# Fillers at a layer boundary, adds moved up in a norm, first loads and last outputs dealt out anew, small columns by tokens

## The reference, cut to what matters

```python
for l in range(2):
    h = rms_norm(x, norm_mix[l])
    proj = h @ w_in[l]                      # 7688 columns; da, db are 4 + 4 of them
    (dq, dk, dv, dz, da, db, mq, mk, mv, lx, ly, gates) = split_columns(proj)
    mixed = g0 * y_deltanet + g1 * y_attention + g2 * y_recurrence
    x = x + mixed @ w_o[l]
    h = rms_norm(x, norm_ffn[l])
    gate, up = jnp.split(h @ ffn_in[l], 2, axis=-1)
    x = x + (jax.nn.silu(gate) * up) @ ffn_down[l]
return rms_norm(x, norm_final)
```

## Time and profile before

| | |
|---|---|
| time, median of 3 runs | 951.11 us (950.91 to 951.41) |
| the profiled execution's own time | 952.0 us |
| its span | 950.2 us |
| TensorE busy | 930.6 us, 98% |
| VectorE / ScalarE busy | 646.4 us / 495.0 us |
| mean granted TensorE clock | 0.994 |
| TensorE stopped on listed waits | 10.4 us in all |

### The profile page before, as it was taken

The page is one execution under the profiler, slowest core; times in us unless marked ns, Lnnn a source line. Parts: engine busy times, 40 slices in busy tenths (PEclk is TensorE's granted clock), DMA queues, the critical chain, the costliest instruction groups (busy, mean ns, idle before and its releaser), DMA issues.

```text
span 950.2 us, 15345 instructions
## 1 busy us (share of the span) xinstructions
PE 930.6 (98%) x6344; PEld 833.7 (88%) x6344; DVE 646.4 (68%) x1026; ACT 495.0 (52%) x837; POOL 2.4 (0%) x6
## 2 busy tenths in 40 slices
PE   7999999999999999999999999999999999999996
PEld 5999899999987888888879998999999788888885
DVE  6889956685767555555678897665858675555555
ACT  6574445775446444444465555467744454444442
POOL 0000000000000000000000000000000000000000
PEclk9999999999999999999999999999999999999999
DMA  8554424446554655565635344344555566555541
GB/s 300 181 169 139 134 93 134 151 161 199 184 188 151 205 189 187 178 200 177 212 127 181 121 139 133 95 149 149 188 178 178 177 199 203 191 183 183 179 146 45
DMA packets 43989, 158.65 MB, mean 167 GB/s; under 512 B 5008, under 2 KB 5264, under 8 KB 43920
## 3 DMA queue, kind: packets, MB, share of 16 engines
q1 hardware_dynamic: 43920, 157.67, 50.3%
HBM read 156.60 MB, written 1.05 MB: 166 GB/s over the span
## 4 chain that ended last, share of the span: by engine, by line
PE 88%; DVE 7%; ACT 3%; DMA 1%; issue 1%; SPq 0%; DVEq 0%; ACTq 0%
PE bank L293 12%; PE bank L294 11%; PE bank L295 11%; PE bank L391 8%; PE bank L389 8%; PE bank L390 8%; PE bank L466 6%; PE bank L333 5%; PE bank L331 5%; PE bank L332 5%; PE bank L431 2%; DVE wlo L984 2%; PE bank L432 1%; PE bank L433 1%; PE bank L404 1%; DVE tmp L1031 1%
## 5 line engine op out<-in xcount | busy, mean ns | idle before, releaser
L707 ACT CAST whi<-raw 128x1024 fp32r<-128x1024 f32 x292 | 305.9, 1050 | 361.0 <-PE bank L295 132.1
L984 DVE TENSOR_TENSOR wlo<-raw,whi 128x1024 fp32r<-128x1024 f32 x292 | 353.2, 1219 | 131.9 <-ACT whi L707 131.3
L293 PE MATMUL bank<-ahi,whi 128*128 128x256 f32 x832 | 239.5, 288 | 0.4
L294 PE MATMUL bank<-alo,whi 128*128 128x256 f32 x832 | 235.3, 283 | 0.0
L295 PE MATMUL bank<-ahi,wlo 128*128 128x256 f32 x832 | 235.3, 283 | 0.0
L293 PEld LDWEIGHTS bank<-ahi,whi 128*128 128x128 f32 x832 | 159.4, 192 | 2.0 <-DVE tmp L1031 0.5
L294 PEld LDWEIGHTS bank<-alo,whi 128*128 128x128 f32 x832 | 159.5, 192 | 0.1
L295 PEld LDWEIGHTS bank<-ahi,wlo 128*128 128x128 f32 x832 | 159.4, 192 | 0.0
L389 PE MATMUL bank<-whi,ahi 128*128 128x512 f32 x320 | 126.5, 395 | 0.0
L391 PE MATMUL bank<-whi,alo 128*128 128x512 f32 x320 | 124.8, 390 | 0.0
L390 PE MATMUL bank<-wlo,ahi 128*128 128x512 f32 x320 | 124.5, 389 | 0.0
(11 more groups left out here) (243 smaller groups left out, 1242.0 us busy)
## 6 DMA issues: line engine op xcount, KB each, us to landing
raw<-stream_dram SPq DMA_DIRECT2D x292, 512.0 KB, 4.1
par<-params_dram SPq DMA_DIRECT2D x2, 568.5 KB, 8.8
x<-x_dram SPq DMA_DIRECT2D x2, 512.0 KB, 5.2
out_dram<-x SPq DMA_DIRECT2D x4, 256.0 KB, 2.2
con<-consts_dram SPq DMA_DIRECT2D x1, 612.0 KB, 9.1
proj<-final_dram SPq DMA_DIRECT2D x1, 512.0 KB, 5.5
ident<-ident_dram SPq DMA_DIRECT2D x1, 64.0 KB, 3.5
rab<-ab_dram SPq DMA_DIRECT2D x1, 64.0 KB, 8.4
```

The lines of the kernel that those rows point to most:

```text
L293: pe.matmul(dst, whi_of(m)[:, wcol], hi, start=first, stop=False, skip_group_check=True)
L294: pe.matmul(dst, whi_of(m)[:, wcol], lo, start=False, stop=False, skip_group_check=True)
L707: act.copy(whi_of(m), raw_of(m)).then_inc(*AC.up(("hi", m), "w"))
L984: dv.tensor_tensor(wlo_of(m), raw_of(m), whi_of(m), ALU.subtract).then_inc(*DV.up(("lo", m), "w"))
```

## The change

- TensorE: six exact products 128 x 128 x 128 on the identity before the first transposes of layer 1, and two after the first transposes of each layer. Their results are not used.
- Mixing norm: ScalarE and VectorE swap their halves of the scaling, so the first four transposes wait for VectorE. Second tokens' transposes go to banks 6 and 7, four to a bank, and are rounded once the bank is full.
- Feed-forward norm: the second tokens' two adds go behind the first two splits of the first tokens. `adds, 2 splits, adds, 6 splits, 8 splits` instead of `adds, 8 splits, adds, 8 splits`.
- First loads: `x` of the first tokens in two transfers, raw 0 behind them, then identity and norm weights as one tensor, then `x` of the second tokens.
- Small columns: `ahi` and `alo` become stationary (128 columns), `wab` moves (16 or 8 columns): 32 products instead of 16, and results stand by tokens. `fold`, its two products and the copy at k = 4 go; VectorE adds the parts at k = 5.
- The values' transposes move from k = 28 to 29, ScalarE's two copies from 29 and 30 to 30 and 31.
- End: the root is cut in steps; the second tokens' adds go behind its first step. GpSimd weighs two halves. ScalarE writes three outputs, VectorE one; the stores' order is changed.

```diff
@@ transfers
-            sp.dma_start(x[:, 0, :], x_in[:, 0, :]).then_inc(loaded_x[0], 16)
-            sp.dma_start(ident[:, :], ident_in).then_inc(loaded_ident, 16)
-            sp.dma_start(nrm[:, :], norms).then_inc(loaded_nrm, 16)
+            for c in range(2):
+                sp.dma_start(x[:, 0, c * 512:(c + 1) * 512], x_in[:, 0, c * 512:(c + 1) * 512]).then_inc(loaded_x[c], 16)
             load(0)
-            sp.dma_start(x[:, 1, :], x_in[:, 1, :]).then_inc(loaded_x[1], 16)
+            sp.dma_start(unit[:, :], unit_in).then_inc(loaded_unit, 16)
+            sp.dma_start(x[:, 1, :], x_in[:, 1, :]).then_inc(loaded_x[2], 16)
...
-            for t, c in ((0, 0), (1, 0), (1, 1), (0, 1)):
+            for t, c in ((0, 0), (0, 1), (1, 1), (1, 0)):
@@ TensorE
+            return bank[6 + kt // 4][:, (kt % 4) * P:(kt % 4 + 1) * P] if t else bank[kt // 2][:, (kt % 2) * P:(kt % 2 + 1) * P]
...
                     elif c == 0:
+                        pe.wait_ge(*DV.at(l, ("xs", t)))
+                    else:
                         pe.wait_ge(*AC.at(l, ("xs", t)))
-                    else:
-                        pe.wait_ge(*DV.at(l, ("xs", t)))
...
-                    for kt in range(KT):
-                        pe.matmul(bank[3][0:16, 0:T], wab[:, kt, :], ahi[:, kt, :], ...)
-                        ins = pe.matmul(bank[3][0:8, 0:T], wab[:, kt, 0:8], alo[:, kt, :], ...)
+                    for t in range(2):
+                        tok = slice(t * P, (t + 1) * P)
+                        for kt in range(KT):
+                            pe.matmul(bank[3][:, 16 * t:16 * t + 16], ahi[:, kt, tok], wab[:, kt, :], ...)
+                            ins = pe.matmul(bank[3][:, 16 * t:16 * t + 8], alo[:, kt, tok], wab[:, kt, 0:8], ...)
...
-                if k == 4:
-                    pe.wait_ge(loaded_con, 16)
-                    pe.wait_ge(*DV.at(l, "abrows"))
-                    for m in range(2):
-                        ins = exact(bank[3][:, T + 8 * m:T + 8 * m + 8], proj[0:16, AB, m * P:(m + 1) * P], c_("fold", 8, slice(0, 16)))
...
-                if k == 28:
+                if k == 29:
                     pe.wait_ge(*AC.at(l, "ssq"))
...
+                if l:
+                    for i in range(6):
+                        exact(bank[3][:, 0:P], ident, ident)
                 x_transpose(l, "mix", 0)
+                for i in range(2):
+                    exact(bank[4][:, 0:P], ident, ident)
@@ ScalarE
-                        act.wait_ge(*PE.at(l, (step, "xT", t, kt // 2)))
+                        act.wait_ge(*PE.at(l, (step, "xT", t, kt // 4 * 2 + 1 if t else kt // 2)))
...
-                if k == 29:
+                if k == 30:
                     act.wait_ge(*PE.at(l, "vT"))
...
-                if k == MV0 + 4:
+                if k == MV0 + 5:
...
+            act.wait_ge(*DV.at(L, ("mix", "nr", 0)))
+            act.wait_ge(*DV.at(L, "xw"))
+            scaled_out(0, 0)
+            act.wait_ge(*PO.at(L, ("xw", 0, 1)))
+            scaled_out(0, 1)
+            act.wait_ge(*DV.at(L, ("mix", "nr", 1)))
+            act.wait_ge(*PO.at(L, ("xw", 1, 0)))
+            scaled_out(1, 0)
@@ VectorE
-                for t in range(2):
-                    for c in range(2):
-                        x_add(l, "ffn", 2 * FFN0 - 1, t, c)
-                    x_split(l, "ffn", 2 * l + 1, t, range(KT))
+                x_add(l, "ffn", 2 * FFN0 - 1, 0, 0)
+                x_add(l, "ffn", 2 * FFN0 - 1, 0, 1)
+                x_split(l, "ffn", 2 * l + 1, 0, (0, 1))
+                x_add(l, "ffn", 2 * FFN0 - 1, 1, 0)
+                x_add(l, "ffn", 2 * FFN0 - 1, 1, 1)
+                x_split(l, "ffn", 2 * l + 1, 0, range(2, KT))
+                x_split(l, "ffn", 2 * l + 1, 1, range(KT))
...
-                weigh(0)
-                root(L, 0)
+                step(dv.tensor_tensor(flat(tiles(XW, 2)), x[:, 0, 0:512], flat(tiles(FINAL, 4))[:, 0:512], ALU.mult), "xw")
+                root_first(L, 0)
+                x_add(L, "mix", NH - 1, 1, 0)
                 x_add(L, "mix", NH - 1, 1, 1)
-                x_add(L, "mix", NH - 1, 1, 0)
+                root_step(L, 0, 12.0)
+                root_step(L, 0, 768.0)
+                root(L, 1)
...
-                if k == 4:
                     dv.wait_ge(*PE.at(l, "ab"))
-                    step(dv.tensor_copy(proj[0:16, AB, :], bank[3][0:16, 0:T]), "abrows")
-                if k == 5:
...
+                    step(dv.tensor_copy(az, ab[:, 1, 0]))
+                    step(dv.tensor_copy(bz, ab[:, 1, 1]))
+                    settle(1)
+                    step(dv.tensor_tensor(az, ab[:, 0, 0], az, ALU.add))
+                    settle(1)
+                    step(dv.tensor_tensor(bz, ab[:, 0, 1], bz, ALU.add))
+                    settle(1)
+                    step(dv.tensor_tensor(az, az, each(p_("dtb", 0, 4), 2), ALU.add))
...
-            dv.wait_ge(loaded_nrm, 16)
+            dv.wait_ge(loaded_unit, 16)
@@ GpSimd
+            po.wait_ge(*DV.at(L, "final"))
+            for t, c in ((0, 1), (1, 0)):
+                cols = slice(c * 512, (c + 1) * 512)
+                po.wait_ge(*DV.at(L, ("mix", "x", t, c)))
+                po.tensor_tensor(flat(tiles(XW + 4 * t + 2 * c, 2)), x[:, t, cols], flat(tiles(FINAL, 4))[:, cols], ALU.mult).then_inc(*PO.up(("xw", t, c)))
```

More of the change, by code:

```diff
@@ L67 @@
 _at = 0
-for _n, _k in [("causal", 128), ("fold", 8), ("cos", 256), ("sin", 256), ("tri", 128), ("eye", 64),
+for _n, _k in [("causal", 128), ("cos", 256), ("sin", 256), ("tri", 128), ("eye", 64),
                ("up1", 64), ("up2", 64), ("up4", 64), ("up8", 64), ("up16", 64), ("up32", 64)]:
@@ L97, in last, with build @@
         return self.sem, self.n - back
-def build(nc, wstream, params, consts, norms, final, x_in, ident_in, ab_in, out, known):
+def build(nc, wstream, params, consts, final, x_in, unit_in, ab_in, out, known):
     ctx = ExitStack()
@@ L135, in build @@
         loaded_raw = [sem(f"loaded_raw{i}") for i in range(RING)]
-        loaded_x = [sem(f"loaded_x{i}") for i in range(2)]
-        loaded_final, loaded_ident = sem("loaded_final"), sem("loaded_ident")
-        loaded_con, loaded_nrm, loaded_par, loaded_ab = (sem(n) for n in ("loaded_con", "loaded_nrm", "loaded_par", "loaded_ab"))
+        loaded_x = [sem(f"loaded_x{i}") for i in range(3)]
+        loaded_final, loaded_unit = sem("loaded_final"), sem("loaded_unit")
+        loaded_con, loaded_par, loaded_ab = (sem(n) for n in ("loaded_con", "loaded_par", "loaded_ab"))
         stored = sem("stored")
@@ L244, in in_copied, with xt_of @@
             return AC, ("in", c)
-        def xt_of(kt):
-            return bank[kt // 2][:, (kt % 2) * T:(kt % 2 + 1) * T]
+        def xt_of(kt, t):
+            return bank[6 + kt // 4][:, (kt % 4) * P:(kt % 4 + 1) * P] if t else bank[kt // 2][:, (kt % 2) * P:(kt % 2 + 1) * P]
         def landed(m):
@@ L282, in _ @@
                         sp.dma_start(flat(tiles(FINAL, 4)), final).then_inc(loaded_final, 16)
-            for t, c in ((0, 0), (1, 0), (1, 1), (0, 1)):
-                sp.wait_ge(*(DV.at(L, ("out", t)) if c else AC.at(L, ("out", t))))
+            for t, c in ((0, 0), (0, 1), (1, 1), (1, 0)):
+                if t and c:
+                    sp.wait_ge(*DV.at(L, "out"))
+                else:
+                    sp.wait_ge(*AC.at(L, ("out", t, c)))
                 sp.dma_start(out[:, t, c * 512:(c + 1) * 512], x[:, t, c * 512:(c + 1) * 512]).then_inc(stored, 16)
@@ L961, in _, with scaled_out @@
             for t in range(2):
-                for c in (range(2), (1, 0))[t]:
+                for c in range(2):
                     act.wait_ge(*DV.at(L, ("mix", "x", t, c)))
                     square(L, t, c)
-                act.wait_ge(*DV.at(L, ("mix", "nr", t)))
-                act.wait_ge(*DV.at(L, ("xw", t)))
-                act.activation(x[:, t, 0:512], flat(tiles(XW + 2 * t, 2)), ACT.Copy,
-                               scale=sm["nr"][:, t:t + 1]).then_inc(*AC.up(("out", t)))
+            def scaled_out(t, c):
+                act.activation(x[:, t, c * 512:(c + 1) * 512], flat(tiles(XW + 4 * t + 2 * c, 2)), ACT.Copy,
+                               scale=sm["nr"][:, t:t + 1]).then_inc(*AC.up(("out", t, c)))
+            act.wait_ge(*DV.at(L, ("mix", "nr", 0)))
[6 more added lines that the diff above has]
+            scaled_out(1, 0)
         @block.vector
@@ L1468, in _constants @@
     put("causal", np.where(q[None, :] <= q[:, None], 0.0, -1e30).astype(np.float32))
-    put("fold", np.tile(np.eye(8, dtype=np.float32), (2, 1)))
     half = HD // 8
@@ L1547 @@
     arrays = {"stream_dram": stream, "params_dram": par, "consts_dram": _constants(),
-              "norms_dram": np.ascontiguousarray(norms), "final_dram": np.ascontiguousarray(final),
-              "x_dram": np.ascontiguousarray(xs), "ident_dram": np.eye(P, dtype=np.float32),
+              "final_dram": np.ascontiguousarray(final),
```

(1 more changed line is left out.)

82 lines of the change are left out of this document (40 added, 42 removed).

## The result

The changed kernel took 954.53 us (median of 8, 953.24 to 957.77) and the kernel before 951.26 (median of 8) on the same chip: a ratio of 1.0036, with a 95% interval of 1.0023 to 1.0049. It is slower by 3.3 us. The forecast was 948.8, the range 945.9 to 950.7, and "slower" had a chance of 0.06.

The account below looks back on a forecast made before the run. TensorE's stream of matmuls, with its stops and slow places, was taken to bound the kernel. The terms +2.2 - 2.0 - 1.3 - 0.2 - 1.0 = -2.3, from the median 951.1, gave 948.8; range 945.9 to 950.7.

Parts of the forecast that it names:

- Small columns: Small-column products at k = 3, both layers: 32 products paced at 0.115 by weight loads, +1.1 a layer, +2.2 in all.
- Rival 4: Small products at k = 3 of each layer: loads don't overlap, 0.192 a product, +7.1, total 953.7, slower; chance 0.06.
- rival 1: Small products: weight loads cheaper, 0.058 a product giving 945.2, 0.085 giving 947.0; taken as 946.2, chance 0.18.
- Layer boundary: TensorE between the layers, once: fillers keep the full clock and swapped scaling starts ScalarE's rounding 0.23 earlier; -1.3.
- The cap of the forecast: Second transposes at the layer boundary: scaled second tokens come only at 483.4, limiting the gain from 484.79 to -1.3.
- Feed-forward norm: Second tokens' transposes, twice: TensorE's wait for adds behind eight splits goes; 2 x 1.02 = -2.0.
- First loads: Program start: norms ride with the identity, landing at 7.6, and halved transposes end 0.45 earlier; -0.2, bounds -0.7 and +0.7.
- End: Program end: second root ends 0.5 earlier, VectorE writes one output, last store issued at 946.3; -1.0, bounds -1.2 and +0.4.
- rival 3: Program end: GpSimd holds up VectorE's root steps, 0.85 at the first root and 0.5 at the second; +1.4, 950.2, chance 0.07.

## Why the prediction was wrong

The measured parts add up, though each is known to some 0.8 only, so that part of the close fit is luck; the swap of the scaling and the fillers at the start were not measured alone. As differences against the kernel before: small columns +4.66, feed-forward order -1.39, fillers -0.25, loads +0.56, end -0.44, in all +3.14; the whole change measured +3.27. The forecast terms were +2.2, -2.0, -1.3, -0.2 and -1.0. The miss, from -2.3 to +3.3, is 2.5 of clock behind the small products, 1.0 at the layer boundary, 0.6 at the feed-forward norm, 0.8 at the first loads and 0.6 at the end.

- **Small columns: the step failed, though its pace was right.** "32 x 0.115 = 3.68, or +1.1 a layer" measured 1.0 a layer by the traces, and +2.16 for both in the medians. Rival 4 (0.192 a product) and rival 1 (0.058) are out. What was missing is a second price: behind such products the granted clock fell to 0.50 for 6.8 us, which cost 2.5 in the median. It took the change from +0.8, with the small products widened and not told from no change, to +3.3. The sum has no term for it. The prediction took "TensorE is busy here without a stop" as cover. It looked for falls only beside idle stretches, while the change cut the moving columns of this place from 256 to 16 and 8.
- **Layer boundary: -1.3 in the profiled pair, -0.25 in the runs.** The fall "at about 478.9" was read from one execution and priced as if every one had it; four other profiles with that gap have none. Even where it falls it costs 0.83 at the second transposes, not the 1.5 of the forecast, since without it TensorE waits there for ScalarE. The cap of the forecast was right: 483.4 for the second transposes; with the swap and no fall they come 7.97 behind the last product, which in the kernel before would be 483.5. (484.79 - 483.4 is 1.4, where the text writes 1.3.) The sum went by that execution, and the step to the runs took off only the 0.9 between it and the median.
- **Feed-forward norm: the mechanism was right and the size was off,** -1.4 for -2.0. The wait on the adds went, but TensorE now waits for the second tokens' first split and, further on, for the split of the next weights, which the forecast did not follow down VectorE's list: -0.74 a layer, not -1.02.
- **First loads: a term of the sum was mis-sized.** "I put the landing at 7.6"; it is 8.1 in the median of nine profiles, and the root behind it is not hidden: +0.6, inside the bounds given.
- **End: rival 3 happened** and should have stood in the sum. It names this pair of engines and the price (0.85 and 0.5; measured 0.74 and 0.52). The forecast's argument that GpSimd "has 1.6 and 3.4 us before anyone needs them" asked who waits for its result, not whom it holds up.

## What to carry to other kernels

Price a change in a product's shape twice: the load it shows (0.11 for 128 stationary columns, wherever a product is too short to cover it) and the moving columns it takes out of TensorE's stream, since a full busy share did not keep the clock. A fall of the clock in one profile is a draw; before paying for its cure, look at the spread of the runs and at a second trace. Work moved to GpSimd was free here only beside VectorE operations that read at most one operand in SBUF. And when work moves up on an engine, follow its list down past the wait that goes: what stood behind it, here the split of the next weights, can be what TensorE waits for next.

## What the hardware showed unexpectedly

A run of 32 products of 16 and 8 moving columns, every 0.11 us and with no gap, was followed by a granted clock of 0.50 in three of four places in two profiles; the same run at 128 columns was not, in either layer. A tiny product set between products of 512 columns cost 0.117, as much as in a run of its own. A one-column operation of VectorE can last 0.90 instead of 0.16. And the gap of 1.3 to 1.5 us at the layer boundary was followed by a fall in one trace and by none in four others.
